# A two-layer block on one core: down products woven into the up products, and sixteen seven-product pairs per layer

## What is computed

```python
def conv_ffn(h, w_up, conv_w, conv_b, w_down):
    Tp = h.shape[1]
    u = h @ w_up
    up = jnp.pad(u, ((0, 0), (CONV_W - 1, 0), (0, 0)))
    c = conv_b + sum(up[:, j:j + Tp] * conv_w[j] for j in range(CONV_W))
    gate, val = jnp.split(c, 2, axis=-1)
    return (jax.nn.silu(gate) * val) @ w_down
...
        h = h + conv_ffn(rms_norm(h, ln_ffn_g[i]), w_up[i], conv_w[i], conv_b[i], w_down[i])
```

## Time and profile before

| what | us |
|---|---|
| median of 3 runs | 2120.32 |
| lowest, highest | 2119.39, 2124.4 |
| the profiled execution, its own time | 2124.43 |
| its span, first to last instruction | 2123.1 |
| PE busy in the span | 2092.9 (99%) |
| DVE, ACT, POOL busy | 1521.6, 1039.1, 189.2 |

### The profile page before, as it was taken

The page is one execution under the profiler, slowest core; times in us unless marked ns, Lnnn a source line. Parts: engine busy times, 40 slices in busy tenths (PEclk is TensorE's granted clock), DMA queues, the critical chain, the costliest instruction groups (busy, mean ns, idle before and its releaser), DMA issues.

```text
span 2123.1 us, 45256 instructions
## 1 busy us (share of the span) xinstructions
PE 2092.9 (99%) x19642; PEld 1841.3 (87%) x19642; DVE 1521.6 (72%) x2562; ACT 1039.1 (49%) x1799; POOL 189.2 (9%) x191
## 2 busy tenths in 40 slices
PE   8999999999999999999999999999999999999999
PEld 2877787878777888898899999999988899999987
DVE  5889888888698766885588888324666667888722
ACT  3235566556442635356565455224666656444411
POOL 0000000000010001364321111000000030000000
PEclk9999999999999999999999999999999999999999
DMA  7641011211255353100177787423111033444231
GB/s 301 130 120 51 3 47 57 77 51 47 105 166 152 119 180 121 60 24 21 48 214 196 217 230 197 137 93 131 61 41 36 21 94 95 121 144 135 92 100 67
DMA packets 72216, 228.32 MB, mean 108 GB/s; under 512 B 8689, under 2 KB 11761, under 8 KB 71569
## 3 DMA queue, kind: packets, MB, share of 16 engines
q1 hardware_dynamic: 63280, 192.38, 28.2%
q0 software_dynamic: 8736, 33.03, 7.0%
HBM read 218.77 MB, written 39.65 MB: 122 GB/s over the span
## 4 chain that ended last, share of the span: by engine, by line
PE 87%; DVE 8%; ACT 3%; DMA 1%; issue 1%; SPq 0%; DVEq 0%; ACTq 0%
PE PS L651 62%; PE PS L1261 7%; PE PS L836 3%; PE PS L825 2%; DVE ca L2257 2%; PE PS L1401 2%; PE PS L1198 2%; PE PS L1369 1%; PE PS L845 1%; PE PS L1171 1%; DVE wlo L2155 1%; DVE Ssc L2674 1%; PE PS L816 1%; PE PS L805 1%; DMA early<-in_wall 1%
## 5 line engine op out<-in xcount | busy, mean ns | idle before, releaser
L1449 ACT ACTIVATE whi<-raw 128x1024 fp32r<-128x1024 f32 (+3 forms) x346 | 329.8, 954 | 255.7 <-PE PS L651 203.1
L2155 DVE TENSOR_TENSOR wlo<-raw,whi 128x1024 fp32r<-128x1024 f32 (+2 forms) x288 | 337.8, 1179 | 114.5 <-ACT whi L1449 114.4
L651 PE MATMUL PS<-nhi,whi 128*128 128x264 f32 (+1 forms) x1616 | 339.8, 291 | 0.3 <-DVE nlo L2523 0.3
L651 PE MATMUL PS<-nhi,wlo 128*128 128x264 f32 (+1 forms) x1616 | 326.9, 284 | 0.4 <-DVE wlo L2155 0.4
L651 PE MATMUL PS<-nlo,whi 128*128 128x264 f32 (+1 forms) x1616 | 327.1, 284 | 0.0
L651 PE MATMUL PS<-hhi,whi 128*128 128x512 f32 x648 | 266.0, 411 | 0.7 <-DVE hlo L2210 0.4
L651 PEld LDWEIGHTS PS<-nhi,whi 128*128 128x128 f32 x1616 | 251.3, 189 | 7.9 <-issue 1.1
L651 PE MATMUL PS<-hhi,wlo 128*128 128x512 f32 x648 | 254.4, 393 | 1.0 <-DVE wlo L2155 0.9
L651 PE MATMUL PS<-hlo,whi 128*128 128x512 f32 x648 | 254.2, 392 | 0.0
L651 PEld LDWEIGHTS PS<-nhi,wlo 128*128 128x128 f32 x1616 | 250.3, 189 | 0.7 <-DVE wlo L2155 0.7
L651 PEld LDWEIGHTS PS<-nlo,whi 128*128 128x128 f32 x1616 | 250.8, 189 | 0.0
(11 more groups left out here) (410 smaller groups left out, 4110.5 us busy)
## 6 DMA issues: line engine op xcount, KB each, us to landing
raw<-in_wall SPq DMA_DIRECT2D x252, 512.0 KB, 3.8
p_rows<-in_wall POOLq DMA_DIRECT2D x14, 1280.0 KB, 7.3
raw<-p_rows SPq DMA_DIRECT2D x28, 512.0 KB, 4.3
early<-in_wall SPq DMA_DIRECT2D x16, 512.0 KB, 14.6
p_rows<-in_wall POOLq DMA_DIRECT2D x28, 256.0 KB, 5.5
p_rows<-p_rows POOLq DMA_DIRECT2D x28, 256.0 KB, 4.9
raw<-in_wall SPq DMA_DIRECT2D x16, 384.0 KB, 3.1
raw<-in_wall SPq DMA_DIRECT2D x20, 256.0 KB, 2.6
```

Source lines behind the costliest of these rows:

```text
L651: q = e.matmul(out, cuts[a][:, k * P:(k + 1) * P], (hi_, lo_)[b][:, kr if b == 0 or what[:4] != "down" else slot_of(kr), lo:lo + w], start ...
L1449: return e.activation(out, src, func, **kw)
L2155: e.tensor_tensor(wlo[slot[i]][:, w], room_of(i)[:, w], whi[slot[i]][:, w].bitcast(F32), ALU.subtract).then_inc(*up("lo_dve", i))
```

## The change

The set of seven-product pairs grows from 7 to 16 in each layer (j = 5, 7 and 8 to 21). The contraction of the down product is cut into three groups of f tiles: 0 to 6, 7 to 14 and 15 to 21. The units of the first two groups, each for one output tile, are woven in, one behind each pair from j = 7 on (and one more after j = 21); DVE adds each partial result to `H` at once. The third group comes last, one unit for each output tile, with the norm work that belonged to the three units. f lives in one array of 45 tiles, in which rooms of group 0 and of the activation sums are used again; the cuts of f are made one pair later, always. The sums of weights are now 32 quads: 6 before the attention of layer 0, 14 at the start of its feed-forward network, 6 at `b_kv` (after the bias table of layer 1 has been set) and 6 at the start of the feed-forward network of layer 1. The scaling of `H` moves into attention steps 8 to 15.

```diff
-SEVENTHS = ((5, 7, 9, 11, 13, 15, 17), (5, 7, 9, 11, 13, 15, 17))
+SEVENTHS = ((5, 7) + tuple(range(8, 22)),) * 2
+GROUPS = ((0, 7), (7, 8), (15, 7))
+def ffn_steps(layer):
+    partial = [("down", j, g) for g in range(2) for j in range(8)]
+    for j in range(22):
+        yield ("sum" if j in SEVENTHS[layer] else "up"), j, None
+        if j >= GROUPS[0][1]:
+            yield partial.pop(0)
+    yield from partial
+    for j in range(8):
+        yield "last", j, 2
...
-        for js in ((0, 1), (2,), (3,), (4,), (5,), (6,), (7,)):
-            for k0, nk in ((0, 8), (8, 8), (16, 6)):
-                for j in js:
-                    units.append((f"down{layer}", j * P, k0, nk))
...
-            fhi.append(grid(blockmem(f"fhi{layer}", 22 * T, F32R), 22))
-            flo.append(grid(blockmem(f"flo{layer}", 23 * T, F32R), 23))
+            blockmem(f"F{layer}", 45 * T)
...
+        def slot_hi(j):
+            return j if j < 14 else 29 if j == 21 else j - 14
+        def slot_lo(j):
+            return 22 + j if j < 7 else 7 + j
+        def slot_free(layer, j):
+            if 14 <= j < 21:
+                return "unit", woven_last[layer]
+            return ("unit", sum_last[layer]) if j == 21 else None
...
-                bank_of = {1: other, 7: other + 1, 3: 7} if again else {1: 4, 7: 7, 3: 4}
-                bank_of.update({2: 5, 6: 6, 5: pair + 1, 4: pair})
+                bank_of = {1: 4, 2: 5, 3: 4, 4: pair, 5: pair + 1, 6: 6, 7: 7}
...
+                    if kind == "down":
+                        n = (T, S)[layer]
+                        full(f"down{layer}", F_cut, F_cut, halves(n, pair_of_banks((f"part{layer}", g, j)), T - n),
+                             (lambda k: on.wait_ge(*at(f"f{layer}", k))) if j == 0 else None, k0=GROUPS[g][0])
+                        continue
...
-                residual(f"down{layer}", f"ffn{layer}", fhi[layer], flo[layer], f"f{layer}", (T, S)[layer], 3)
+                residual(f"down{layer}", f"ffn{layer}", F_cut, F_cut, f"f{layer}", (T, S)[layer], first=GROUPS[2][0])
...
+                    f_upper(j)
                     ahead(count.take() + 3)
                     tap0(j, 1)
                     tap0(j, 0)
-                    if j + 1 in SEVENTHS[layer]:
-                        ahead(count.next + 3)
+                    ahead(count.next + 3)
                     gate(j)
...
+                    f_lower(j)
                     i = count.take()
                     on.wait_ge(*at("unit", i))
                     e.tensor_tensor(gate_2, PS[:, bank_of[3], 0:w], gate_2, ALU.add).then_inc(*up("M3", layer, j))
...
                     taps(j, 1)
+                    ahead(i + 4)
                     taps(j, 0)
                     gated(j)
...
+                    if kind == "down":
+                        b, i, n = a_pair(), passed(), (T, S)[layer]
+                        ahead(count.next + 3)
+                        on.wait_ge(*at("unit", i))
+                        h_ = sv(H[:, j, T - n:], n)
+                        e.tensor_tensor(h_, psv(n, b), h_, ALU.add).then_inc(*up(f"part{layer}", g, j))
+                        continue
...
-            sums(0, 3)
+            sums(0, 6)
...
-                    next(scaling, None)
...
+                    if 8 <= n < 16:
+                        next(scaling)
...
-            sums(3, len(quads))
+            sums(6, 20)
             while units[count.next][0] != "b_kv":
                 passed()
             on.wait_ge(s_tz, 32)
             e.memset(TZ[0:64, :, T - 64:T], NEG).then_inc(*up("TZ", 1))
+            sums(20, 26)
+            while units[count.next][0] != "up1":
+                passed()
+            sums(26, len(quads))
```

More of the change, by code:

```diff
@@ L547, in build @@
             LO.append("lo_pool" if what in ON_POOL and (what, base) not in HANDED_OVER else "lo_dve")
+        sum_last = [max(i for i, u in enumerate(units) if u[0] == f"sum{layer}") for layer in range(2)]
+        woven_last = [max(i for i, u in enumerate(units) if u[0] == f"down{layer}" and u[2:] == GROUPS[0]) for layer in range(2)]
         tail = n
@@ L650, in product @@
                         for n, (out, lo, w) in enumerate(outs):
[L651 removed]
+                            q = e.matmul(out, cuts[a][:, k * P:(k + 1) * P], (hi_, lo_)[b][:, (slot_hi, slot_lo)[b](kr) if what[:4] == "down" else kr, lo:lo + w],
                                          start=start and k == 0 and a == b == 0, stop=stop and k == nk - 1 and a == 1)
@@ L1281, in sevenths @@
                 i = begin()
-                if again:
-                    on.wait_ge(*at("M126", layer, j - 1))
                 block(i, 0, 6, made(1))
-                bank_free(pair, ("M45", layer, j))
+                assert pair_of_banks(("M45", layer, j)) == pair
                 block(i, 1, 5, made(0)).then_inc(*up("unit", i))
@@ L1908, in residual @@
                 for j in range(8):
-                    for _ in range({0: 5, 1: 1}.get(j, 3) if n_units == 3 else 1):
-                        passed()
+                    passed()
                     if n == S:
@@ L1973, in sevenths @@
                     tap0(j, 0)
-                    if j + 1 in SEVENTHS[layer]:
-                        ahead(count.next + 3)
+                    ahead(count.next + 3)
                     gate(j)
-                for j in range(22):
-                    if j in SEVENTHS[layer]:
+                for kind, j, _ in ffn_steps(layer):
+                    if kind == "sum":
                         sevenths(j)
-                        last_sum = count.next - 1
                         continue
+                    if kind == "down":
+                        passed()
+                        continue
+                    if kind == "last":
+                        break
                     normed()
@@ L2772, in residual @@
                     b = a_pair()
-                    for _ in range({0: 4, 1: 0}.get(j, 2) if n_units == 3 else 0):
-                        passed()
                     i = count.take()
```

96 lines of the change are left out of this document (42 added, 54 removed).

## The result

| | before | change |
|---|---|---|
| median, runs side by side | 2120.56 us (4 runs) | 2092.82 us (4 runs) |
| lowest, highest | 2119.39, 2124.4 | 2090.53, 2093.4 |
| ratio, 95% interval | | 0.9864 (0.9847 to 0.9881) |
| the profiled execution, its span | 2124.43, 2123.1 | 2090.53, 2089.2 |

The change saves 27.7 us, or 1.4%. The forecast was 23.5 us. The median lies 4.2 us under the predicted 2097.0 and 0.2 us under the low end of the range, 2093.

A forecast was written before the change was run, and what follows sets the result against it. PE was taken to bound both feed-forward networks. 26.1 us of matmuls saved, less 2.1 of stall and 0.5 for the scaling, gave 23.5 off the median 2120.32: 2097 us, range 2093 to 2111.

The forecast's parts named there:

- The chain to u3's `wlo`: Feed-forward step: from one u3's end to the next u3's rounding `wlo`, 12.3 us in layer 0, 12.2 in layer 1.
- both margins: Feed-forward step: `wlo` ready before PE needs it, by 0.3 us in layer 0 and 0.1 us in layer 1.
- the ends of the weave: First woven unit and last group in each network: no stall; if f21 came late, 1 us once per layer.
- Rival 1: Feed-forward step becomes DVE's, the chain being longer than added up: +12.6 us, about 2107, up to 2112; chance 0.20.
- Rival 2: Quads over 28.8 us each in layer 0 hold SyncE's loads and starve PE: 2169 at 36 us each; chance 0.03.
- Rival 3: Attention: the moved scaling's bias waits pass through to PE, up to 10 us, 2105; chance 0.06.
- Rival 4: Feed-forward networks: no gain, something else paces them or small bubbles eat it, about 2118; chance 0.03.
- matmuls removed: Both feed-forward networks: nine more pairs save 108 matmuls per layer, 13.11 us in layer 0 and 12.96 in layer 1.
- stall in layer 1: Feed-forward network of layer 1: PE waits 0.15 us per step over 14 steps, 2.1 us.
- scaling of `H`: Eight POOL operations moved into the busier attention: cost 0.5 us, bounds nothing and 10 us.
- The price of a matmul: Feed-forward networks, from marks: 0.1214 us in layer 0; in layer 1 0.1200, and 0.2320 in down with 512 columns.
- The quads: Sums made ahead on POOL: 24.8 us each early, 25.4 in the network, 34 us to spare in layer 0.

The follow-up runs named there:

- doubled combinations: The change with extra M7 or M45 work on DVE per seven-product pair: 0.46 us added 2095.89 us, 0.73 us 2100.85, 1.46 us 2122.58.
- second M7: The changed kernel with M7 of each seven-product pair done twice on DVE, 0.46 us more per step: 2095.89 us, ratio 0.9867.
- three M45: The changed kernel with M45 of each seven-product pair done three times, 1.46 us more per step: 2122.58 us, ratio 0.9995.
- run with late quads: The changed kernel with three quads before the attention instead of six, 17 at the start of the first network: 2128.98 us, ratio 1.0025.

## What of the prediction held, and what failed

**What held.** That PE alone sets both networks, that 216 matmuls go, and what a step takes: 15.28 and 14.89 us, where 15.30 and 14.95 were forecast. The chain to u3's `wlo` held to a few hundredths, and so did both margins (0.28 and 0.09, forecast 0.3 and 0.1), which the doubled combinations measured. No group was late at the ends of the weave. Nothing of the DVE work that the change adds reached PE.

**The rivals.** Rival 1 (the step becomes DVE's) didn't happen, but is 0.1 us away in layer 1; the runs with added work show that a step over its margin grows by the excess, as I had it. But only 8 of the 13 distances per layer are that tight; I had counted 14 alike, and those with units of eight blocks have 0.9 to 1.0 us. Rival 2 (quads late) didn't happen; the run with three quads early shows it, with a price of 37.6 us in one layer. Rival 3 (the moved scaling stalls the attention) is wrong: the stretch with the scaling takes 93.11 us, and 93.17 without. Rival 4 (no gain) is wrong.

**What failed, by its terms:**

| term of the sum | forecast | measured |
|---|---|---|
| matmuls removed | -26.1 | -26.8, both networks between their marks |
| stall in layer 1 | +2.1 | about 0 (PE's list has no wait there) |
| scaling of `H` | +0.5 | -3.4 |
| attention of layer 1 | nothing | +0.2 |
| sum | -23.5 | -30.0 by marks, -27.7 by medians |

- **The scaling of H** is the step that failed. I priced the place that it goes to, and nothing for the place that it leaves, "where POOL idled". The range for it was "nothing, and 10 us": I excluded a gain without a reason. POOL had time there, but DVE had not, and the two hinder each other: the scaling's eight operations held DVE's `Ssc` rows by 3.8 us. The rows were in the trace before: `Ssc` with 272 columns at 1382 ns beside 767 for 528.
- **The stall** was a guard, not a reading: my own chain gave a margin of 0.1 us in layer 1, and I put 0.15 us of wait on top of it. PE waited for nothing. These two terms are what the sum missed: without them it is -26.1 us, and 2094, and with the 3.4 us of the scaling 2091; the median of 2092.8 lies between, and by itself it could not tell which term was off. The marks do.
- **The price of a matmul** in layer 1 was an average. By the change's marks the seven-product pair there costs 14.89 - 4.87 = 10.02 us for 84, 0.1193 each, so that the plain pair beside it before took 21.60 - 10.02 = 11.58, and a pair replaced saves 1.56 us and not 1.44. For nine pairs that is 1.1 us, of which 0.6 is lost again somewhere (9 x 1.56 = 14.1, measured 13.5). The two marks above, 2086.48 - 2081.61, are the 4.87.
- **The quads** were mis-sized too, 25.4 for 27.9 us, at no cost. Two causes were open: a fuller DVE, or more traffic. With the second M7 DVE was busier still (104.56 of 115 us from 1220 on, against 102.48) and the ten quads took 26.3 us each; with three M45 they took 26.2. So a fuller DVE doesn't lengthen them. The prediction had weighed a rule of the Trainium skill ("SBUF — State Buffer", section "Who interferes with whom") in two halves, and that speaks for the second, which the page calls inferred. Whether traffic does, stays open: the change has a DMA share of 0.81 between 1220 and 1343 us, and the kernel before 0.78 in its quads of 1200 to 1351, while the same code scatters from 26.2 to 27.9.
- **The low end** of the range was the full saving and 1 us. It left no room for any term to be better than priced, and that is where the median fell.

What stays open: what takes back the 0.6 us in layer 1, whether 0.8 us more ahead of the attention are the change's, and whether and why the quads are longer.

## What to carry to other kernels

When an operation is moved from one place to another, price both places, and the one that it leaves even if its own engine idled there: look on the other engines for short instructions that last longer than long ones of the same kind. Where two changes come together, one that makes work scarce on the bound engine and one that gives the second engine room, each can lose alone and both can win; the room is what to compute, per step and to the tenth of a microsecond, and it is worth measuring by doubling a small instruction. A transfer that is made ahead has a due time, and a limit per transfer (here 28.8 us) that can be written down before the run: see how near the measured one comes, not only that nobody waits.

## What was not expected of the hardware

- DVE instructions lasted longer beside POOL's work on SBUF, seen as a longer row and not as a wait before it: one of 0.64 us took 1.48 beside a scaling, and one of 0.43 us, with a single tensor as input, 2.25 beside a rounding. The `Ssc` row of 272 columns took 1382 ns on average before, 1071 without the scaling, 790 without four of the roundings too.
- In the run with late quads the granted clock fell although PE was still busy four fifths of the time. Its stretches:

```profile
1250.00:1300.00 50.00, 50.00 (x415) 50.00 (x414) 44.96 (x62) 25.09 (x34) 6.75 (x9) 1.00 0.79 229
1300.00:1350.00 50.00, 42.58 (x306) 41.34 (x306) 32.11 (x47) 17.54 (x22) 8.38 (x11) 0.90 0.70 192
1350.00:1400.00 50.00, 38.57 (x274) 37.50 (x274) 28.95 (x39) 16.42 (x21) 7.59 (x10) 0.86 0.69 192
1400.00:1432.00 32.00, 26.75 (x203) 26.23 (x201) 20.34 (x28) 10.67 (x14) 4.71 (x7) 0.89 0.82 248
```

PE had been busy without a hole until 1300 at 1.00 (2.4 GHz). From there it stood 24.1 us of 132, in five places, and the mean granted clock was 0.90 and 0.86, so that part of the time was at 1.2 GHz. The late weights are thus paid for twice. Of the 37.6 us, PE's waits in the list (21.5 for `whi`, 2.6 for `wlo`) are 24.1, which leaves 13.5. An estimate from the last three rows: their 783 matmuls took 107.90 us of busy time, and at 0.1214 each they would take 95.1, so 12.8 us are the clock's. The run with seventeen pairs paid in the same way for waits of only 1.8 us.
